# A hybrid decoder step: causal convolution in channel-major projection tiles, and gates and memory queries inside the last tiles

## The chip, the cores and the metric

One core of a Trainium2 chip runs the whole kernel. The time is that of one execution on the device, in microseconds (us). TensorE (PE) multiplies, VectorE (DVE), ScalarE (ACT) and GpSimd (POOL) work on elements, SyncE (SP) only issues transfers; ScalarE and GpSimd issue transfers too. The engines run side by side, each strictly in its own order, and wait for one another by semaphores.

## The reference

One layer of a decoder step, for a prompt of 512 rows and for 32 sample rows (8 sequences of 4 tokens). Cut to what matters here:

```
z = rms_norm(x) @ w_in              # 2048 columns in; split into the groups below
# (A) mLSTM, 4 heads of 256: q and k go through a short convolution over time
m_qk, m_v, m_o, m_gate, m_if = ...  # 2048, 1024, 1024, 1024 and 8 columns
y[t, c] = b[c] + sum_j w[j, c] * m_qk[t - 3 + j, c]     # 4 taps, per channel
qk = silu(y);  p_conv = last 3 rows of m_qk             # an output
ig = m_if[:, :4] + b_if;  lf = log_sigmoid(m_if[:, 4:] + b_if)
# per head: weights of every pair of rows from the running sum of lf and its running
# maximum with ig; num = (q k^T * weights) v + carried state; normalised, * sigmoid(m_o)
# (B) sparse attention, 4 heads of 128, with an index that selects keys per query
# (C) attention into 256 memory tokens, 4 heads of 128: queries c_q, gate c_gate
mix = concat(m_out * silu(m_gate), a_out * silu(a_gate), c_out * silu(c_gate))
out = x + rms_norm(mix @ w_out)
```

The sample rows go through the same with cached keys, memory keys and values (8 sequences of 256 tokens) and carried states.

## The kernel before

**Tiles.** `tensor_tile` makes 512 columns of `z` at a time: two tiles of the memory's keys and values, then the columns behind the mLSTM group (first group), then the 10 tiles of `w_in`'s first 5120 columns (second group, N_B0 to N_Y0: q and k of the convolution in tiles 1 to 4, v 5 and 6, o 7 and 8, gate 9 and 10), and at the end the output projection. A tile has 8 chunks of 256 input rows. For each chunk ScalarE casts the weights to a high part (`w_hi`, L385) when the chunk two before is used, GpSimd makes the low part (`w_lo`, L389), and TensorE adds three products for each k and block of 128 rows (L431 to L433; two for the sample rows, L426 and L427): the rows of x stand, the weights move, so a block is row-major. ScalarE scales the finished blocks by the row's norm and stores them to `z_prompt` and `z_sample` in memory.

**Hosted work.** While TensorE runs the second group it also does the sparse attention. `tensor_prompt` (the prompt's index, selection and attention) and `tensor_gather` (the sample rows; L991 is the row sum) are generators: `tensor_tile` takes a step of `steps[0]` in the middle and at the end of a chunk, and one of `steps[1]` at its end, ahead of that of `steps[0]`. `scalar_tile` does the same once a chunk, behind its cast, one piece behind TensorE. VectorE runs 80 iterations, one for each chunk: a step of the prompt, one of the rows, one of the prompt. The prompt's steps end early in the tenth tile.

**Behind the tiles** comes, in this order: attention into memory for the samples (`*_mem_s`: the queries from `z_sample`, the sum of their two parts at L1348, a cleared `q_spread`, then per sequence key transposes L1397 and logits L1409, softmax, values L1424). `beside_memory` sets the four parts of `*_mlstm_gates` between its steps (i and f transposed, ScalarE's Exp and Ln at L1581 and L1583, VectorE's sums and running maxima L1610 to L1625, and the turn of the convolution's weights). Their constants are loaded by `sync_mlstm_consts`. Next is the convolution of head 0, then what the samples need (`*_mlstm_s_prep`, loads from L1921), then the four heads. In the loop of head h stand also the state pairs of the samples (`side`; in heads 1 to 3) and the four units of the convolution of head h + 1:

```
side(0)
if h + 1 < H:
    tensor_conv_turn(pe, h + 1, i)      # 4 transposes of 128x128 into CONV (L1655)
side(1)
```

A unit is 128 channels by 512 rows. `vector_conv` takes the four taps from PSUM (L1667, L1669), `scalar_conv` the Silu (L1681), each with a table load ahead of it, because the head's other functions stand in another table. `sync_mlstm_head` loads five blocks of 512 KB for each head: q, k, o, gate, v.

Memory key and value pages (512 KB) are loaded by GpSimd (`gpsimd_mem_in`) into three buffers, from the end of the tenth tile on.

## Time and profile before

| what | value |
|---|---|
| median of 3 runs | 1882.44 us (1881.62 to 1884.41) |
| the profiled execution's own time | 1877.01 us |
| its span (first to last instruction) | 1875.3 us |
| mean granted clock of TensorE | 0.937 of full speed |
| TensorE busy | 1679.8 us, 90% |
| VectorE, ScalarE, GpSimd busy | 814.8, 569.1, 673.4 us |

All times of rows are in us from the span's start. The second group runs from about 624 to 1256.4, memory attention to 1325.5, head 0's convolution and the samples' start to 1350.8, the heads from there to 1595, the output projection from 1647.5 to 1845. A row of the timeline has the start, the duration, engine, line and operation, output and inputs, and in brackets how long the engine was idle before and what released it. "x16" counts instructions.

### The profile page before, as it was taken

To read this page: it belongs to the slowest core of one execution; us is meant where nothing else is said; L and a number is where in the kernel's file an instruction comes from. 1 tells how busy PE (TensorE), PEld (TensorE's weight loads), DVE (VectorE), ACT (ScalarE), POOL (GpSimd) and SP (SyncE) were. 2 spreads that over 40 slices of the span, in tenths; PEclk is the share of its full clock that TensorE was granted. 3 is DMA by queue.
4 is the path that set the end of the run, shared out by engine and by line. 5 is a ranking of instruction groups with operands and counts; after the bars stand their busy time and mean duration, and the time that the engine had idled before them with its cause. 6 is when DMAs were issued, how large, how long until landed. Compare 5 with 4: busy or idle time off the path is not lost.

```text
span 1875.3 us, 20980 instructions
## 1 busy us (share of the span) xinstructions
PE 1679.8 (90%) x7801; PEld 1272.0 (68%) x7801; DVE 814.8 (43%) x1319; ACT 569.1 (30%) x876; POOL 673.4 (36%) x448
## 2 busy tenths in 40 slices
PE   6899999999999499998899999987658789799995
PEld 5677775677897376776688778865334455477774
DVE  6400010599929856755632161112465454501113
ACT  5522233222221233233222422224244443312221
POOL 3655531333333166766444444421110111033331
PEclk9999999999999699999999999998667788789997
DMA  6544431233344267766455544437404323542222
GB/s 214 160 134 130 142 101 56 71 105 108 92 120 144 77 196 231 221 197 211 122 154 165 149 134 117 147 125 230 93 29 152 107 68 107 192 160 85 83 78 106
DMA packets 139674, 249.01 MB, mean 133 GB/s; under 512 B 26504, under 2 KB 63308, under 8 KB 136296
## 3 DMA queue, kind: packets, MB, share of 16 engines
q10 hardware_dynamic: 66928, 122.86, 21.0%
q1 hardware_dynamic: 55920, 72.76, 12.2%
q0 software_dynamic: 16736, 52.18, 9.6%
q8 instruction: 58, 0.95, 0.2%
q14 instruction: 32, 0.26, 0.0%
HBM read 204.11 MB, written 43.66 MB: 132 GB/s over the span
## 4 chain that ended last, share of the span: by engine, by line
PE 73%; DVE 13%; DMA 5%; ACT 4%; issue 2%; POOL 1%; ACTq 1%; SPq 0%; DVEq 0%; POOLq 0%
PE acc L431 16%; PE acc L433 16%; PE acc L432 16%; PE acc L426 4%; PE acc L427 4%; PE ps_c L991 3%; PE acc L1722 2%; DVE arena L1669 1%; PE ps_c L2116 1%; PE acc L2111 1%; DMA arena<-z_prompt 1%; PE ps_a L1155 1%; POOL w_lo L389 1%; ACT z_tile L471 1%; PE ps_a L1224 1%
## 5 line engine op out<-in xcount | busy, mean ns | idle before, releaser
L389 POOL TENSOR_TENSOR w_lo<-w_raw,w_hi 128x1024 fp32r<-128x1024 f32 (+1 forms) x200 | 466.7, 2334 | 814.8 <-ACT w_hi L385 814.5
L431 PE MATMUL acc<-w_hi,x_hi 128*128 128x512 f32 (+1 forms) x1472 | 580.4, 394 | 8.8 <-DVE keep L925 5.3
L433 PE MATMUL acc<-w_hi,x_lo 128*128 128x512 f32 (+1 forms) x1472 | 565.9, 384 | 0.0
L432 PE MATMUL acc<-w_lo,x_hi 128*128 128x512 f32 (+1 forms) x1472 | 565.3, 384 | 0.0
L385 ACT CAST w_hi<-w_raw 128x1024 fp32r<-128x1024 f32 (+1 forms) x200 | 204.2, 1021 | 758.3 <-PE acc L427 716.6
L431 PEld LDWEIGHTS acc<-w_hi,x_hi 128*128 128x128 f32 x1472 | 278.8, 189 | 93.9 <-issue 28.0
L433 PEld LDWEIGHTS acc<-w_hi,x_lo 128*128 128x128 f32 x1472 | 278.1, 189 | 55.8
L432 PEld LDWEIGHTS acc<-w_lo,x_hi 128*128 128x128 f32 x1472 | 278.8, 189 | 51.4 <-issue 0.7
L426 PE MATMUL acc<-w_hi,x_hi 128*64 128x512 f32 (+1 forms) x368 | 141.4, 385 | 0.0
L427 PE MATMUL acc<-w_lo,x_hi 128*64 128x512 f32 (+1 forms) x368 | 140.9, 384 | 0.0
L2231 DVE TENSOR_TENSOR arena<-arena (+1 forms) x16 | 14.0, 887 | 176.8 <-ACT arena L464 176.8
L471 ACT ACTIVATE z_tile<-acc,small 128x512 f32<-128x512 f32 (+3 forms) x95 | 63.6, 669 | 48.3 <-PE acc L433 32.1
L881 POOL DMA_INDIRECT arena<-in_cache_attn_k,keep x64 | 67.4, 1054 | 19.5 <-issue 19.5
L795 DVE MAX8 keep<-arena 32x8 f32<-32x2052 f32 x32 | 73.2, 2286 | 1.1
L796 DVE FIND_INDEX8 arena<-keep,arena 32x8 uint32<-32x2052 f32 x32 | 72.9, 2277 | 0.0
L797 DVE MATCH_REPLACE8 arena<-keep,arena 32x2052 f32<-32x2052 f32 x32 | 72.6, 2268 | 0.0
L427 PEld LDWEIGHTS acc<-w_lo,x_hi 128*64 128x64 f32 x368 | 49.5, 134 | 31.5 <-issue 0.2
L657 DVE TENSOR_TENSOR arena<-arena 32x1104 f32<-32x1104 f32 x1 | 1.3, 1297 | 158.3 <-DMA arena<-z_sample 158.3
L881 POOL DMA_INDIRECT arena<-in_cache_attn_v,keep x64 | 62.2, 972 | 14.5 <-issue 11.6
L426 PEld LDWEIGHTS acc<-w_hi,x_hi 128*64 128x64 f32 x368 | 49.5, 135 | 23.6 <-issue 0.2
L991 PEld LDWEIGHTS ps_c<-arena 128*128 128x128 f32 x512 | 62.1, 192 | 4.4
L991 PE MATMUL ps_c<-arena 128*128 128x1 f32 x512 | 58.9, 245 | 0.0
(439 smaller groups left out, 1903.0 us busy)
## 6 DMA issues: line engine op xcount, KB each, us to landing
w_raw<-in_w_in ACTq DMA_DIRECT2D x136, 512.0 KB, 3.7
z_prompt<-z_tile ACTq DMA_DIRECT2D x68, 256.0 KB, 2.5
w_raw<-in_w_out ACTq DMA_DIRECT2D x32, 512.0 KB, 3.6
arena<-z_prompt SPq DMA_DIRECT2D x4, 2088.0 KB, 10.2
w_raw<-in_w_mem_kv ACTq DMA_DIRECT2D x16, 512.0 KB, 4.1
arena<-q_sample POOLq DMA_DIRECT2D x32, 256.0 KB, 4.0
arena<-z_prompt SPq DMA_DIRECT2D x10, 512.0 KB, 7.3
between<-z_prompt SPq DMA_DIRECT2D x10, 512.0 KB, 10.1
```

What stands on the lines that cost most here:

```text
L385: nc.scalar.copy(w_hi[:, c % 2, :, 0:w], w_raw[:, c % RAWS, :, 0:w]).then_inc(chunk_hi, 1)
L389: nc.gpsimd.tensor_tensor(out=w_lo[:, c % 2, :, 0:w], in0=w_raw[:, c % RAWS, :, 0:w], in1=w_hi[:, c % 2, :, 0:w].bitcast(F32), op=ALU.subt ...
L426: nc.tensor.matmul(acc[m][0:2 * R, 0:w], xs, wh, start=first, stop=False)
L427: last = nc.tensor.matmul(acc[m][0:2 * R, 0:w], xs, wl, start=False, stop=end)
L431: nc.tensor.matmul(acc[m][:, 0:w], xh, wh, start=first, stop=False)
L432: nc.tensor.matmul(acc[m][:, 0:w], xh, wl, start=False, stop=False)
L433: last = nc.tensor.matmul(acc[m][:, 0:w], xl, wh, start=False, stop=end)
L471: nc.scalar.activation(z_tile[0:rows, m, 0:w], acc[m][0:rows, 0:w], ACT.Copy, scale=rstd(NU_MEM + m, rows)).then_inc(acc_read, 1)
L795: dlink(nc.vector.max(top8, score))
L796: dlink(nc.vector.max_index(sel_idx[:, 8 * i:8 * i + 8], top8, score))
L881: pool.indirect_dma_start(out=got_v[s][:, c, :], out_offset=None, in_=v_rows if values else k_rows, in_offset=bass.IndirectOffsetOnAxis(ap ...
L991: last = nc.tensor.matmul(ps_c[:, PC_O + h * R + r:PC_O + h * R + r + 1], got_v[s][:, c, h * AD:(h + 1) * AD], probs_t[:, c, h, r:r + 1], ...
```

## The change

It computes the four q and k tiles as fifth to eighth of the second group, and channel-major: the weights stand, x moves, and a block is 128 channels by 512 rows. ScalarE copies such a block and doesn't store it. In the first four iterations of the next tile VectorE scales it by the row norms (broadcast over the partitions by `tensor_late_consts` once, after the third tile of the first group), keeps the last three columns for `p_conv` and applies the taps in place (`vector_conv`). ScalarE takes the four Silu of a tile and stores them to `qk_p` at the seventh chunk (`late`). The heads load q and k from there, and have no convolution any more.

The gates and the sum, transposes and spreading of the memory queries go into the tenth tile: TensorE's first gate part after the second chunk, the queries' transposes after the fourth, the last gate part after the seventh; ScalarE's four parts at its chunks 3, 5, 6 and 8. Their loads are issued by SP as soon as the prompt's attention is stored. VectorE runs the gates, then the queries, then the end of the gathered rows. The first two pages of memory keys go to the buffer of the prompt's memory keys and values, and are issued once GpSimd is done with the casts. The loads of head 0's v, o and gate wait until the memory keys are used, since `q_spread` now lies there. `p_conv` is stored from SBUF in six transfers of single elements.

```diff
+    NCT = 2 * MW // TN
+    B_ORDER = (4, 5, 6, 7, 0, 1, 2, 3, 8, 9)
+    CT0 = B_ORDER.index(0)
...
+        qk_p = scratch("qk_prompt", [2 * MW, S])
...
-                return w_in_v, TN * (n - N_B0)
+                return w_in_v, TN * B_ORDER[n - N_B0]
...
+                            if kind == "t":
+                                xh, xl = hi_t[:, k, 0:S], lo_t[:, k, :]
+                                wh, wl = (v[:, c % 2, i, m * P:(m + 1) * P] for v in (w_hi, w_lo))
+                                nc.tensor.matmul(acc[m][:, :], wh, xh, start=first, stop=False)
+                                nc.tensor.matmul(acc[m][:, :], wl, xh, start=False, stop=False)
+                                last = nc.tensor.matmul(acc[m][:, :], wh, xl, start=False, stop=end)
+                                continue
...
+                if kind == "t" and m < MT:
+                    nc.scalar.copy(z_tile[:, m, :], acc[m][:, :]).then_inc(acc_read, 1)
+                    continue
...
+                if c == CH - 2 and late is not None:
+                    late()
...
+            for dst, src in ((conv_nat[0:CK, :], I["conv_w"][0]), (conv_nat[CK:CK + 1, :], I["conv_b"][0:1, :])):
+                sp.dma_start(dst, src).then_inc(tables_in, 16)
...
+        def tensor_late_consts(pe):
+            pe.wait_ge(*at("rstd_spread"))
+            pe.wait_ge(tables_in, 16 * N_TABLES)
+            for m in range(MT):
+                nc.tensor.matmul(ps_c[:, m * P:(m + 1) * P], conv_a[:, m * P:(m + 1) * P], ident[:, :], start=True, stop=True)
+            for k in range(KT):
+                last = nc.tensor.transpose(ps_b[:, k * (CK + 1):(k + 1) * (CK + 1)], conv_nat[:, k * P:(k + 1) * P],
+                                           ident[0:CK + 1, 0:CK + 1])
+            last.then_inc(reached("late_turned"), 1)
+
+        def vector_late_consts(dve):
+            dve.wait_ge(rstd_ready, 2)
+            for m in range(MT):
+                last = nc.vector.tensor_copy(conv_a[:, m * P:(m + 1) * P], rstd(NU_MEM + m, P).broadcast_to([P, P]))
+            last.then_inc(reached("rstd_spread"), 1)
+            dve.wait_ge(*at("late_turned"))
+            nc.vector.tensor_copy(rstd_bc, ps_c[:, :])
+            nc.vector.tensor_copy(conv_c, ps_b[:, 0:KT * (CK + 1)].rearrange("p (k j) -> p k j", j=CK + 1)
+                                  ).then_inc(reached("late_copied"), 1)
+            dve.wait_ge(*at("late_copied"))
...
+        def vector_conv(dve, i, m):
+
+            k = 4 * i + m
+            dve.wait_ge(acc_read, acc_base(N_B0 + CT0 + i) + m + 1)
+            dlink(nc.vector.tensor_tensor(out=conv_a, in0=z_tile[:, m, :], in1=rstd_bc, op=ALU.mult))
+            nc.vector.tensor_copy(last_rows(k // 8)[:, k % 8, :], conv_a[:, S - CK + 1:S])
+            out = z_tile[:, m, :]
+            dlink(nc.vector.tensor_scalar(out, conv_a, conv_c[:, k, CK - 1:CK], None, ALU.mult))
+            for j in range(1, CK):
+                ins = nc.vector.scalar_tensor_tensor(out=out[:, j:S], in0=conv_a[:, 0:S - j],
+                                                     scalar=conv_c[:, k, CK - 1 - j:CK - j], in1=out[:, j:S],
+                                                     op0=ALU.mult, op1=ALU.add)
+                if j < CK - 1:
+                    dlink(ins)
+            ins.then_inc(cv_tapped, 1)
+            dve.wait_ge(cv_tapped, k + 1)
+
+        def scalar_conv(act, i):
+
+            for m in range(MT):
+                k = 4 * i + m
+                act.wait_ge(cv_tapped, k + 1)
+                nc.scalar.activation(z_tile[:, m, :], z_tile[:, m, :], ACT.Silu, bias=conv_c[:, k, CK:CK + 1]).then_inc(cv_silu, 1)
+            for m in range(MT):
+                k = 4 * i + m
+                act.wait_ge(cv_silu, k + 1)
+                act.dma_start(qk_p[k * P:(k + 1) * P, :], z_tile[:, m, :]).then_inc(z_stored[m], 16)
 
...
+        cq_in = place(X_OFF, [2, AW], R)
+        cq_low = place(10 * (S + R) + 13324, [2, AW], R)
+        q_spread = place(10 * (S + R), [H * NB * (P + NQ)])
+        k_mem = [mem_kv[:, :, 0:AW], mem_kv[:, :, AW:2 * AW], part(xh_free, 4224, [NMEM // P, AW])]
...
 
         def gpsimd_mem_in(pool):
-            pool.wait_ge(chunk_used, CH * N_Y0)
-            pool.dma_start(cq_in, z_s[0:R, C_CQ:C_CQ + 2 * AW].rearrange("r (a c) -> r a c", a=2)).then_inc(cq_loaded, 16)
-            pool.dma_start(cq_low, z_s[R:2 * R, C_CQ:C_CQ + 2 * AW].rearrange("r (a c) -> r a c", a=2)).then_inc(cq_loaded, 16)
+            pool.wait_ge(o_stored, 16 * 2 * MT)
+            pool.wait_ge(mem_out, 16 * 2 * NMEM // P)
             for i in range(2 * NB):
                 b = i % NB
+                if i == 2:
+                    pool.wait_ge(chunk_used, CH * N_Y0)
...
             dve.wait_ge(cq_loaded, 32)
-            for m in range(MT + 1):
-                dve.wait_ge(z_stored[m], 16 * (N_Y0 - N_A0))
             nc.vector.tensor_tensor(out=cq_in, in0=cq_in, in1=cq_low, op=ALU.add).then_inc(reached("cq_ready"), 1)
-            nc.vector.memset(q_spread, 0.0)
-            for t in range(2):
-                dlink(nc.vector.memset(p_spread[t], 0.0))
+            dlink(nc.vector.memset(q_spread, 0.0))
             dve.wait_ge(*at("cq_ready"))
             for h in range(H):
                 last = nc.vector.tensor_copy(gate_c[h * R:(h + 1) * R, :], cq_in[:, 1, h * AD:(h + 1) * AD])
@@ -1357,6 +1430,10 @@
             nc.vector.tensor_copy(q_spread.rearrange("p (i x) -> p i x", x=P + NQ)[:, :, 0:NQ],
...
+            for m in range(MT + 1):
+                dve.wait_ge(z_stored[m], 16 * (N_Y0 - N_A0))
+            for t in range(2):
+                dlink(nc.vector.memset(p_spread[t], 0.0))
...
         def tensor_mem_s(pe):
             pe.wait_ge(*at("cq_ready"))
+            pe.wait_ge(g_copied, 5)
             for h in range(H):
                 last = nc.tensor.transpose(ps_a[:, h * R:(h + 1) * R], cq_in[:, 0, h * AD:(h + 1) * AD], ident[0:R, 0:R])
...
+            pe.wait_ge(*at("g_cols"))
...
+                if b == 0:
+                    pe.wait_ge(*at("mixed_s"))
...
-            act.wait_ge(*at("gate_c_in"))
-            nc.scalar.activation(gate_c, gate_c, ACT.Silu).then_inc(reached("gate_c_ready"), 1)
-            yield
...
+            act.wait_ge(*at("gate_c_in"))
+            nc.scalar.activation(gate_c, gate_c, ACT.Silu).then_inc(reached("gate_c_ready"), 1)
...
+        head_rows = sb("head_rows", [P, H * P])
+        hr = head_rows[0:H, :]
+        rstd_bc = head_rows[:, :]
+
+        z_h = [place(M0, [2, MT, MD]), part(xl_free, 0, [2, MT, MD])]
...
 
         def sync_mlstm_consts(sp):
-            sp.wait_ge(mix_stored, 16 * H)
             sp.wait_ge(o_stored, 16 * 2 * MT)
             sp.wait_ge(kv_stored, 48 * MT)
-            for i in range(MT + 1):
-                sp.wait_ge(z_stored[i], 16 * (N_Y0 - N_A0))
+            sp.wait_ge(cv_tapped, 4 * NCT)
+            sp.dma_start(cq_in, z_s[0:R, C_CQ:C_CQ + 2 * AW].rearrange("r (a c) -> r a c", a=2)).then_inc(cq_loaded, 16)
+            sp.dma_start(cq_low, z_s[R:2 * R, C_CQ:C_CQ + 2 * AW].rearrange("r (a c) -> r a c", a=2)).then_inc(cq_loaded, 16)
...
                              (batch_of, C["batch_of"]), (causal, C["causal"]),
-                             (hn, I["mlstm_head_norm"][0:1, :].broadcast_to([P, MW])),
-                             (conv_nat[0:CK, :], I["conv_w"][0]), (conv_nat[CK:CK + 1, :], I["conv_b"][0:1, :]),
                              (ifp, z_p[:, C_IF:C_IF + 2 * H].rearrange("(m p) c -> p m c", p=P)),
...
-            sp.dma_start(O["p_conv"].rearrange("l b j c -> (l b j) c"), z_p[S - CK + 1:S, 0:2 * MW]).then_inc(conv_out, 16)
+
+        def sync_conv_state(sp):
+            sp.wait_ge(cv_tapped, 4 * NCT)
+            for half in range(2):
+                for j in range(CK - 1):
+                    sp.dma_start(O["p_conv"][0, 0, j, half * MW:(half + 1) * MW].rearrange("(k p) -> p k", p=P),
+                                 last_rows(half)[:, :, j], allow_slow_non_contiguous=True).then_inc(conv_out, 16)
...
         def sync_mlstm_head(sp, h):
             if h == 0:
-                sp.wait_ge(chunk_used, CH * N_Y0)
+                sp.wait_ge(*at("mixed_s"))
+                for i in range(MT + 1):
+                    sp.wait_ge(z_stored[i], 16 * (N_Y0 - N_A0))
             if h >= 2:
                 sp.wait_ge(c_done, 2 * (h - 1))
                 sp.wait_ge(h_out, h - 1)
-            for i, c in enumerate((C_QK, C_QK + MW, C_O, C_G, C_V)):
+            for i in range(2):
+                src = qk_p[i * MW + h * MD:i * MW + (h + 1) * MD, :].rearrange("(d p) t -> p d t", p=P)
+                sp.dma_start(qk_t[h % 2][:, i, :, :], src).then_inc(zh_in[h % 2], 16)
+            if h == 0:
+                sp.wait_ge(cl_used, NB)
+                sp.dma_start(hn, I["mlstm_head_norm"][0:1, :].broadcast_to([P, MW])).then_inc(hn_in, 16)
+            for i, c in enumerate((C_V, C_O, C_G)):
                 src = z_p[:, c + h * MD:c + (h + 1) * MD].rearrange("(m p) c -> p m c", p=P)
-                dst = va[h % 2][:, :, 0:MD] if i == 4 else z_h[h % 2][:, i, :, :]
+                dst = va[h % 2][:, :, 0:MD] if i == 0 else z_h[h % 2][:, i - 1, :, :]
                 sp.dma_start(dst, src).then_inc(zh_in[h % 2], 16)
 
...
-        GATES = acc[0:3]
+        GATES = (ps_a, ps_b, ps_a)
...
+            pe.wait_ge(g_copied, 1)
...
-            pe.wait_ge(g_copied, 5)
-            for k in range(KT):
-                last = nc.tensor.transpose(GATES[0][:, k * (CK + 1):(k + 1) * (CK + 1)], conv_nat[:, k * P:(k + 1) * P],
-                                           ident[0:CK + 1, 0:CK + 1])
-            last.then_inc(reached("conv_w_t"), 1)
-            yield
...
-            pe.wait_ge(conv_silu, 4 * (h + 1))
+            pe.wait_ge(zh_in[h % 2], zh_count(h))
...
-                if h + 1 < H:
-                    tensor_conv_turn(pe, h + 1, i)
...
-                if h + 1 < H:
-                    vector_conv(dve, h + 1, i)
...
-                if h + 1 < H:
-                    scalar_conv(act, h + 1, i)
...
+        def tile_kind(n):
+            return "t" if B_ORDER[n - N_B0] < NCT else "b"
...
+        GATE_GAPS = (4, 3, 3)
+
+        def spaced(pieces, gaps):
+
+            next(pieces)
+            for g in gaps:
+                yield from hosted_pause(g)
+                next(pieces)
+            yield from pieces
...
                 sync_prompt_out(sp, m)
+            sync_mlstm_consts(sp)
+            sync_conv_state(sp)
             sp.wait_ge(*at("mixed_s"))
             store_mix_s(sp, o_s, MW)
-            sync_mlstm_consts(sp)
...
-            steps = (chain(hosted_pause(1), scalar_prompt(act)), chain(hosted_pause(1), scalar_gather(act)))
+            steps = (chain(hosted_pause(1), scalar_prompt(act), hosted_pause(2), spaced(scalar_mlstm_gates(act), GATE_GAPS)),
+                     chain(hosted_pause(1), scalar_gather(act)))
             for n in range(N_B0, N_Y0):
-                scalar_tile(act, n, "b", steps)
+                i = n - N_B0
+                scalar_tile(act, n, tile_kind(n), steps,
+                            late=(lambda i=i: scalar_conv(act, i - CT0 - 1)) if CT0 < i <= CT0 + NCT else None)
             run(steps[0])
             run(steps[1])
-            beside_memory(scalar_mem_s(act), scalar_mlstm_gates(act), (4, 6, 8, 9))
-            for u in range(4):
-                scalar_conv(act, 0, u)
+            run(scalar_mem_s(act))
...
-            for _ in range(CH * NBT):
+            for i in range(CH * NBT):
                 next(prompt, None)
                 next(rows, None)
                 next(prompt, None)
+                t = i // CH - CT0 - 1
+                if 0 <= t < NCT and i % CH < MT:
+                    vector_conv(dve, t, i % CH)
             run(prompt)
             run(rows)
-            vector_gather_out(dve)
+            vector_mlstm_gates(dve)
             mem_s = vector_mem_s(dve)
             next(mem_s)
-            vector_mlstm_gates(dve)
+            vector_gather_out(dve)
             run(mem_s)
-            for u in range(4):
-                vector_conv(dve, 0, u)
             prep, pairs = vector_mlstm_s_prep(dve), vector_mlstm_s(dve)
             next(prep)
             for h in range(H):
...
+            tensor_late_consts(pe)
...
-            steps = (tensor_prompt(pe), chain(tensor_rows(pe), tensor_gather(pe)))
+            mem_s = tensor_mem_s(pe)
+            gates = tensor_mlstm_gates(pe)
+
+            def gates_and_queries():
+                next(gates)
+                yield from hosted_pause(GATE_GAPS[0])
+                next(mem_s)
+                yield from hosted_pause(sum(GATE_GAPS[1:]))
+                yield from gates
+            steps = (chain(tensor_prompt(pe), hosted_pause(2), gates_and_queries()), chain(tensor_rows(pe), tensor_gather(pe)))
             for n in range(N_B0, N_Y0):
-                tensor_tile(pe, n, "b", steps)
+                tensor_tile(pe, n, tile_kind(n), steps)
             run(steps[0])
             run(steps[1])
             tensor_gather_out(pe)
-            beside_memory(tensor_mem_s(pe), tensor_mlstm_gates(pe), (4, 6, 9))
-            for u in range(4):
-                tensor_conv_turn(pe, 0, u)
+            run(mem_s)
```

## Rows read from the trace of the kernel before

**Rows 1.** The page, part 4: the chain, shares by engine

```profile
PE 73%; DVE 13%; DMA 5%; ACT 4%; issue 2%; POOL 1%; ACTq 1%; SPq 0%; DVEq 0%; POOLq 0%
```

**Rows 2.** Stretches behind the tiles: busy time of each engine, clock, transfers

```profile
core 0: us, PE busy (x) PEld busy (x) DVE busy (x) ACT busy (x) POOL busy (x), PEclk, DMA share, GB/s
1256.40:1269.80 13.40, 0.87 (x6) 0.50 (x5) 9.88 (x15) 2.27 (x3) 3.29 (x5) 0.70 0.55 185
1269.80:1305.00 35.20, 29.82 (x173) 24.71 (x173) 8.81 (x22) 19.30 (x41) 5.69 (x8) 0.87 0.85 285
...
1325.50:1350.80 25.30, 11.35 (x26) 5.25 (x26) 17.56 (x21) 5.85 (x9) 0.00 (x0) 0.53 0.44 64
1350.80:1391.10 40.30, 18.37 (x111) 14.29 (x112) 24.47 (x53) 18.20 (x21) 3.57 (x9) 0.58 0.17 52
1406.40:1461.00 54.60, 40.49 (x147) 22.10 (x147) 32.43 (x65) 23.42 (x39) 0.00 (x0) 0.80 0.45 140
1476.30:1529.60 53.30, 40.01 (x143) 21.36 (x143) 31.21 (x61) 23.26 (x39) 0.00 (x0) 0.79 0.45 143
1544.70:1580.30 35.60, 30.55 (x127) 15.90 (x127) 19.82 (x45) 13.65 (x29) 0.00 (x0) 0.94 0.46 140
```

**Rows 3.** Groups by line and shape on VectorE, 1325 to 1600

```profile
L1667 DVE TENSOR_SCALAR arena<-acc,keep_m 128x512 f32<-128x512 f32 x16 | 12.0, 750 | 33.8 <-PE acc L1655 33.7
L1669 DVE SCALAR_TENSOR_TENSOR arena<-acc,keep_m,arena 128x511 f32<-128x511 f32 x16 | 12.0, 750 | 0.6
```

**Rows 4.** Timeline of the gate chain and of the sum of the queries

```profile
1291.30 0.66 ACT L1581 ACTIVATE arena<-arena 4x544 f32<-4x544 f32 x1
1291.97 1.28 ACT L1583 ACT_TABLE_LOAD   x1
...
1293.96 0.71 DVE L1610 SCALAR_TENSOR_TENSOR arena<-arena 4x544 f32<-4x544 f32 x1 [9.10 <-ACT arena L1583]
...
1299.91 0.15 DVE L1625 TENSOR_TENSOR keep_m<-keep_m,arena 4x8 f32<-4x8 f32 x1
...
1260.53 1.21 DVE L1348 TENSOR_TENSOR between<-between 32x1024 f32<-32x1024 f32 x1 [1.62 <-DMA z_sample<-z_tile]
```

**Rows 5.** The sample's loads: issue, time to landing, VectorE's wait

```profile
1328.44 0.33 SPq L1921 DMA_DIRECT2D between<-z_sample  x1
...
between<-z_sample SPq DMA_DIRECT2D x1, 640.0 KB, 9.7
...
1347.94 2.81 DVE L1967 TENSOR_TENSOR between<-between,z_tile 32x2560 f32<-32x2560 f32 x1 [3.69 <-DMA z_tile<-z_sample]
```

**Rows 6.** Timeline of the tenth tile: row sum, ScalarE's next cast

```profile
1227.23 1.84 PE L991 MATMUL ps_c<-arena 128*128 128x1 f32 x16
...
1227.84 1.04 ACT L385 CAST w_hi<-w_raw 128x1024 fp32r<-128x1024 f32 x1 [7.14 <-PE acc L427]
```

**Rows 7.** Waits in the ten tiles: total, times, longest

```profile
DVE keep_p L1275 <- PE ps_c L1232: 66.9, 23, 4.3
...
DVE arena L1288 <- PE ps_a L1224: 43.8, 4, 25.5
```

**Rows 8.** TensorE behind a stall, and the granted clock there

```profile
922.96 0.80 PE L431 MATMUL acc<-w_hi,x_hi 128*128 128x512 f32 x1 [5.25 <-DVE keep L925]
...
924.00:926.00 2.00, 2.00 (x6) 1.61 (x5) 1.86 (x7) 0.00 (x0) 0.27 (x1) 0.50 0.69 199
926.00:928.00 2.00, 2.00 (x7) 1.57 (x7) 1.90 (x5) 0.00 (x0) 0.00 (x0) 0.68 0.08 33
```

**Rows 9.** Waits in head 1

```profile
PE acc L1655 <- DMA arena<-z_prompt: 3.7, 1, 3.7
```

**Rows 10.** Timeline of L1186 with and without a GpSimd cast

```profile
726.99 0.48 DVE L1186 SCALAR_TENSOR_TENSOR arena<-arena,keep_p 128x256 f32<-128x256 f32 x1
...
730.47 2.96 DVE L1186 SCALAR_TENSOR_TENSOR arena<-arena,keep_p 128x256 f32<-128x256 f32 x2 [0.48 <-ACT arena L1168]
...
730.24 2.39 POOL L389 TENSOR_TENSOR w_lo<-w_raw,w_hi 128x1024 fp32r<-128x1024 f32 x1 [2.32 <-ACT w_hi L385]
```

More of the change, by code:

```diff
@@ L58, in hybrid_decoder_step @@
     NBT = C_IF // TN
+    NCT = 2 * MW // TN
+    B_ORDER = (4, 5, 6, 7, 0, 1, 2, 3, 8, 9)
+    CT0 = B_ORDER.index(0)
+    assert len(B_ORDER) == NBT and B_ORDER[CT0:CT0 + NCT] == tuple(range(NCT))
     N_Y0 = N_B0 + NBT
@@ L566, in hybrid_decoder_step @@
         gate_s = keep[:, 912:1040]
+        CK = 4
+        conv_nat = place(X_OFF, [2 * MW], CK + 1)
+        conv_a = place(X_OFF + 3112, [S])
+        conv_c = conv_cols[:, :].rearrange("p (k j) -> p k j", j=CK + 1)
+        last_rows = lambda half: small[:, 32 * half:32 * half + 24].rearrange("p (k j) -> p k j", j=CK - 1)
         POOL_PAGES = 2 * CH * IXT
@@ L1315, in part @@
                                                   **dict(zip(names, shape)))
-        cq_in, cq_low = (part(between, X_HI_N + X_LO_N + i * W_N + W_N // 2, [2, AW])[0:R] for i in range(2))
-        q_spread = part(xh_free, 0, [H * NB * (P + NQ)])
-        k_mem = [part(xh_free, 4224, [NMEM // P, AW]), part(xh_free, 5248, [NMEM // P, AW]),
-                 w_raw[:, RAWS - 1, :, :]]
+        cq_in = place(X_OFF, [2, AW], R)
+        cq_low = place(10 * (S + R) + 13324, [2, AW], R)
+        q_spread = place(10 * (S + R), [H * NB * (P + NQ)])
+        k_mem = [mem_kv[:, :, 0:AW], mem_kv[:, :, AW:2 * AW], part(xh_free, 4224, [NMEM // P, AW])]
         KS = len(k_mem)
@@ L1324, in hybrid_decoder_step @@
         o_c = part(xh_free, 8320 + 2 * NMEM, [AD])
-        gate_c = part(xh_free, 8320 + 2 * NMEM + AD, [AD])
+        gate_c = place(10 * (S + R) + H * NB * (P + NQ), [AD])
         p_spread = [part(zt_free, i * 1056, [NB * (P + NQ)]) for i in range(2)]
@@ L1462, in hybrid_decoder_step @@
         c_e = keep_m[:, 40:60].rearrange("p (m h) -> p m h", h=H)
[L1463 to L1475 removed]
+        mx_T = keep_m[0:H, 60:70]
+        bias_g = keep_m[0:H, 70:72]
+        m0_s = keep_m[0:H, 72:80]
+        a_T = keep_m[0:H, 80:88]
+        bn_o = keep_m[:, 88:96]
+        st_m = keep_m[:, 96:104]
+        aT8 = keep_m[0:NB, 104:108]
+        w_b = keep_m[0:R, 108:140].rearrange("p (h b) -> p h b", h=H)
+        batch_of = keep_m[0:R, 140:148]
+        head_rows = sb("head_rows", [P, H * P])
+        hr = head_rows[0:H, :]
+        rstd_bc = head_rows[:, :]
+        z_h = [place(M0, [2, MT, MD]), part(xl_free, 0, [2, MT, MD])]
         va = [place(M0 + 5120, [MT, MD + 2]), part(xl_free, 4096, [MT, MD + 2])]
         qk_t = [place(M0 + 7180, [2, 2, S]), part(xl_free, 5128, [2, 2, S])]
[L1478 removed]
         k_n = place(M0 + 9228, [MT, MD])
@@ L1488, in hybrid_decoder_step @@
         n_o = place(M0 + 14860, [MD], 1)
-        causal = place(M0 + 15116, [P])
+        causal = place(M0 + 6152, [P])
         assert M0 + 15244 <= AR_N
-        conv_nat = place(M0 + 10252, [2 * MW], CK + 1)
         ifp = place(M0 + 12300, [MT, 2 * H])
@@ L1494, in hybrid_decoder_step @@
         m0_nat = place(M0 + 12396, [H], NB)
-        (mc_in, xc_turned, xc_done, kn_turned, kn_done) = (
-            sem(n) for n in ("mc_in", "xc_turned", "xc_done", "kn_turned", "kn_done"))
+        (mc_in, kn_turned, kn_done) = (
+            sem(n) for n in ("mc_in", "kn_turned", "kn_done"))
         (g_turned, g_copied, mb_done, w_arg, w_exp, s_done, w_done, h_done, gates_mixed, h_sqrt,
@@ L1576, in scalar_mlstm_gates @@
             yield
-            act.wait_ge(*at("conv_w_t"))
-            nc.scalar.copy(conv_c, GATES[0][:, 0:KT * (CK + 1)].rearrange("p (k j) -> p k j", j=CK + 1)).then_inc(reached("conv_w_c"), 1)
             act.wait_ge(*at("g_abs"))
@@ L1804, in vector_mlstm_head @@
             dve.wait_ge(gates_mixed, 2 * (h + 1))
-            nc.vector.tensor_tensor(out=h_o, in0=h_o, in1=z_h[h % 2][:, 2, :, :], op=ALU.mult).then_inc(h_out, 1)
-        conv_silu = sem("conv_silu")
+            nc.vector.tensor_tensor(out=h_o, in0=h_o, in1=z_h[h % 2][:, 0, :, :], op=ALU.mult).then_inc(h_out, 1)
         var_m = sem("var_m")
@@ L2264, in run @@
                 pass
-        def beside_memory(mem_s, gates, places):
-            for i, _ in enumerate(mem_s):
-                if i in places:
-                    next(gates)
-            run(gates)
+        GATE_GAPS = (4, 3, 3)
[5 more added lines that the diff above has]
+            yield from pieces
         def beside_head(h, prep, pairs):
@@ L2453, in _ @@
             vector_rstd(dve, NU_MEM, NU_NORM)
+            vector_late_consts(dve)
             vector_index_prep(dve)
```

98 lines of the change are left out of this document (25 added, 73 removed).

## The prediction

> **What bounds the kernel now.** I read the views in this order: the chain that ended last, the stretches behind the tiles, the operations in them, then waits and single operations.
>
> The chain is TensorE's for 73% of the span and VectorE's for 13% [rows 1]. In the input-projection tiles TensorE is never idle for long, so anything added there on TensorE, or waited for there, is paid in full. From the end of the tenth tile (1256.4 us) to 1580 it is different [rows 2]. In the first 13.4 us TensorE works 0.87 us: it waits for the store of the sample rows, the queries' load and a clearing. In the 25.3 us from 1325.5 it works 11.4, VectorE 17.6. Heads 1 and 2 (each cut from its first product, L1691, to its L1722, the products with v) take 54.6 and 53.3 us; head 3, which has no next head to convolve, takes 35.6, with as many bytes per us and the same two state pairs beside it. The difference is the convolution: each unit has one L1667 and three L1669 on VectorE, 0.75 us each [rows 3], 3.0 us, between transposes and a Silu with a table load. The granted clock is .53 and .58 in the two stretches up to 1391 and .94 in head 3.
>
> **What the change takes out behind the tiles.**
>
> *Memory attention.* The first key transposes can start at the tile's end, since queries and two pages are there: 13.4 us earlier. In the keys and the softmax (35.2 us to 1305) stands the gate chain, now in the last tile. I take 8 us for it and for the two pages already in: the operations of [rows 4] from Exp to L1625 run in this stretch. Against this, value pages will meet the loads of the heads, which are now held until the keys are done. Least: the 13.4 alone. Most: 13.4 + 15.6, the 35.2 cut to the 19.3 that ScalarE is busy in it. I take -21.5 (-13 to -29).
>
> *Head 0's convolution and the sample's start.* The convolution from 1325.5 (25.3 less the 9.3 below: 16 us) goes, but not its time. The loads of the sample's rows are issued at 1328.4, 2.9 us behind the end of memory attention, and take 9.7 us [rows 5]; today they land under the convolution. Then come two VectorE products of 2.8 with a load between them (3.7 waited): 9.3. So 2.9 + 9.7 + about 1.6 for what is issued behind (a load one us later) + 9.3 = 23.5, against 25.3: -1.8 (0 to -9, if the loads land in the 3.7).
>
> *Head 0.* Its stretch from 1350.8 to L1722, 40.3 us, hosts four units of head 1. Each puts 3.0 us on VectorE and one ScalarE table load of 1.28 [rows 4] on the exchange: 4 x 4.3 = -17.3 (-12 by VectorE alone, -25 if transposes, Silu and load back count too).
>
> *Heads 1 and 2* become head 3: 54.6 - 35.6 = -19.0 and 53.3 - 35.6 = -17.7 (-12 each, by VectorE alone). Head 3, the last pairs and the output tiles stay.
>
> Sum: -77.3.
>
> **What it puts into the tiles.**
>
> *The products themselves.* A channel-major tile has the same three products per k and block, at the same width: 0. The order of tiles alone: 0.
>
> *Constants after the third tile.* 20 small products. Sixteen one-column products of L991 take 1.84 us [rows 6]; 20 at that price are +2.3.
>
> *Convolution, 16 units.* Per unit a product, a first tap and three more taps, each 512 wide (0.75 at that width, [rows 3]), and a copy of three columns: about 3.8 us of VectorE, four in each of four tiles, behind the second prompt step of an iteration. Tiles six and eight have the idle time after top-k: VectorE waits there 43.8 us in four waits [rows 7], against 8 x 3.8 = 30. In the other two tiles VectorE waits for TensorE once in each attention step, 66.9 us in 23 waits, 2.9 each [rows 7], and the unit mostly fits. ScalarE's four Silu and stores come at the seventh chunk, some 7 us with two loads, and ScalarE stands idle 7.14 ahead of a cast [rows 6]. Only in the last such tile do they fall amid an attention step: +2.5 for all of it (0 to 20).
>
> *Gates, first part* (end of the second chunk of the last tile): eleven transposes at 0.115 and a turn to ScalarE and back (0.66): +2.5 (1 to 4).
>
> *Memory queries* (end of the fourth chunk). TensorE must wait for the queries' sum, which stands on VectorE behind all of the gate chain, and that behind Ln on ScalarE, which is issued behind the cast that waits for this very chunk. In times of before: the cast ends at 1228.9 [rows 6], Exp 0.66, load 1.28, Ln 0.66 [rows 4], to 1231.5; VectorE's L1610 to L1625 from 1293.96 to 1300.06, 6.1; the sum 1.21: 1238.8. TensorE has the row sum until 1228.9 as cover. So it stands +10 us (0 if the order came out otherwise, 13 with an Exp load). Behind it wait the next chunk and, through it, ScalarE's casts and GpSimd's; nothing in that chain is needed by the wait, so there is no deadlock. Four transposes: +0.6. Gates' last part: ten, +1.1.
>
> *Clock.* After a stall of 5.25 us in an earlier tile TensorE was back at 922.96, with a granted clock of .50, the 1.2 GHz level, until 926 and of .68 in the two us to 928, so 1.00 from about 927.3 [rows 8]: 4.3 us at half, 2.2 lost. After the 10 us above: +2.5 (2 to 5).
>
> Sum: +21.5. GpSimd's page issues and SP's constants, queries and six stores of the convolution's state are moved into the tenth tile, where both queues stand idle; the price of SP's stores of single elements isn't in the trace, but the heads' loads behind them wait for the tile's end anyway: 0.
>
> **Sum.** 1877.0 - 77.3 + 21.5 = 1821.2 for an execution like the profiled one. The median of the runs shown is 5.4 above that: 1827.
>
> **The rivals.** Main case as above, 1827.
>
> *A: the stall is hidden* (VectorE and ScalarE come out ahead of TensorE at the fourth chunk). 12.5 less: 1814. Against it: the cast waits for that chunk by its order.
>
> *B: heads don't become head 3.* Another exchange (state pairs, ScalarE's table loads, or the next head's loads, for which head 1 waits 3.7 us even now [rows 9]) fills what the convolution leaves. Half of the heads' 54.0 us is lost: 1854. For it: head 3 loads nothing for a next head, so its length leaves that out.
>
> *C: VectorE is slowed by GpSimd in the tiles.* Two L1186 that began just behind a GpSimd cast took 2.96 us; one without it took 0.48 [rows 10]. The last three taps and the scaling read two operands from SBUF as L1186 does, where the old taps read PSUM. If each unit in the two tiles of attention takes one such block (2.96 - 2 x 0.48 = 2.0), it is 5.8 us long, against an idle time of 2.9: 8 x 2.9 = 23 us come to TensorE, so 1850. The Trainium skill, "SBUF — State Buffer", section "Who interferes with whom", says that a VectorE instruction with two SBUF inputs contends with a GpSimd instruction that reads SBUF, and it would speak against the new place of the taps; the two L1186 agree.
>
> *D, the other side: the units stand on TensorE's path.* An iteration's next prompt step waits behind the unit on VectorE, and TensorE waits for it in every hosted piece. Then 16 x 3.8 = 61 us come into the tiles, with the block of C 16 x 5.8 = 93: 1888 to 1920, and the change is slower. It decides from 55.8/16 = 3.5 us of each unit on. For it: VectorE runs in order. Against it: the 43.8 us of idle time cover half of the units.
>
> That the change doesn't do what it says would mean that the heads keep their length altogether (B in full, 54 us lost: 1881, no change).
>
> **How the numbers follow.** Main .46, A .14, B .18 and in full .03, C .11, D .08. A measurement of this kernel tells 0.2% (3.8 us) from no change. Faster: main, A, B, C: .89; same .03; slower .08. The range runs from 1804 (A with the larger gain in memory attention) to 1862 (beyond B and C), and leaves out D, B in full and the corners.
>
> **What the profile after would show.** No transposes and taps in the heads; L1691 to L1722 near 36 us in heads 1 and 2, and a higher clock there. First key transposes at the tile's end, memory attention done some 48 us behind it. In the tenth tile one TensorE wait of about 10 us for the queries' sum, at half clock behind it. Taps of 0.7 in tiles six to nine, some of them 2 us and more beside a cast. The prediction is wrong if tiles six to nine grow by more than 10 us together, if the heads stay above 45, or if the fourth chunk shows no wait.

## The result, and the profile after

The changed kernel takes 1836.45 us (four runs, 1833.49 to 1841.48) against 1883.43 (1881.62 to 1886.33): a ratio of 0.9752, 95% interval 0.9723 to 0.9781. The prediction was 1827, with 1804 to 1862, so it is inside the range and 9 us above the likeliest value. The profiled execution took 1841.48 us, its span 1839.8. Line numbers after the change are higher: L390 is ScalarE's cast (L385 before), L1463 transposes the queries, L1423 is their sum, L1732 a head's first product (L1691 before), L1761 the products with v (L1722), L1604 the stores of the convolution's state.

The stretches that answer to [rows 2], cut at the same events: end of the tenth tile, first value product, end of memory attention, first product of the samples, head 0's L1761, then heads 1, 2 and 3 from L1732 to L1761.

```profile
core 0: us, PE busy (x) PEld busy (x) DVE busy (x) ACT busy (x) POOL busy (x), PEclk, DMA share, GB/s
1288.00:1313.90 25.90, 22.02 (x132) 18.76 (x130) 5.56 (x14) 10.93 (x20) 6.51 (x9) 1.00 0.80 262
1313.90:1338.20 24.30, 19.04 (x38) 7.41 (x38) 1.51 (x6) 0.54 (x2) 3.61 (x5) 0.86 0.83 284
1338.20:1361.90 23.70, 4.70 (x9) 1.68 (x8) 5.59 (x3) 2.96 (x5) 0.00 (x0) 0.53 0.47 68
1361.90:1387.70 25.80, 15.91 (x94) 12.59 (x94) 13.45 (x37) 12.77 (x16) 3.57 (x9) 0.58 0.27 81
1401.30:1438.60 37.30, 32.28 (x130) 16.83 (x130) 21.11 (x50) 13.67 (x29) 0.00 (x0) 0.91 0.64 204
1452.70:1494.40 41.70, 36.62 (x127) 18.45 (x127) 19.86 (x45) 13.73 (x29) 0.00 (x0) 0.78 0.59 183
1509.60:1545.20 35.60, 30.57 (x126) 15.85 (x126) 19.83 (x45) 13.59 (x29) 0.00 (x0) 0.94 0.45 140
```

Against before: memory attention takes 50.2 us from the tile's end (69.1 before: 13.4, 35.2, and 20.5 for the values to 1325.5), the samples' start 23.7 (25.3), head 0 25.8 (40.3), head 1 37.3 (54.6), head 2 41.7 (53.3), head 3 the same. With the stretches between heads (1.7 and 1.2 shorter) the tail wins 66.8 us. The tenth tile ends at 1288.0 in place of 1256.4, so the tiles and what is ahead of them give back 31.6. The rest, 35.2, is nearly all of the 35.5 us between the spans of the two profiled executions. The medians are 47 apart: this execution is 5 above its median, that of before 6 below.

Where they give it back is in TensorE's waits; a wait has its sum, count and longest:

```profile
PE ps_a L1463 <- DVE arena L1423: 15.0, 1, 15.0
...
PE acc L439 <- DVE keep L1001: 10.7, 1, 10.7
...
PE ps_a L1636 <- DVE arena L1687: 2.4, 1, 2.4
```

The first is the predicted wait for the queries' sum, 15.0 us in place of 10. The second stood at 5.25 before [rows 8]. The timelines of ScalarE, SP and TensorE around the first:

```profile
1246.66 1.04 ACT L390 CAST w_hi<-w_raw 128x1024 fp32r<-128x1024 f32 x1 [12.50 <-DMA w_raw<-in_w_in]
1247.61 0.65 ACT L1663 ACTIVATE arena<-arena 4x544 f32<-4x544 f32 x1
...
1216.43 29.84 SPq L1604 DMA_DIRECT2D out_p_conv<-small  x6
...
1257.56 0.64 PE L1463 MATMUL ps_a<-ident,arena 32*128 32x32 f32 x4 [15.03 <-DVE arena L1423]
```

The cast ahead of Exp waits for its weights, where that of [rows 6] waited for TensorE, while SP is 29.84 us at six stores of 4 KB each. In these us (the transfers' view of 1216 to 1248: packets, MB, share of 16 engines; then KB and us to landing) weights land 18.6 us after they were asked for; 3.7 is the median of the whole profile:

```profile
q1 hardware_dynamic: 5020, 0.13, 28.1%
...
w_raw<-in_w_in ACTq DMA_DIRECT2D x3, 512.0 KB, 18.6
```

### The profile page after: what moved, and what is told of

Same layout as the page of the kernel before. It is cut to its first block, busy times and chain, and to the rows that moved or that the text cites. A ratio compares the mean times of both kernels' runs of the same rounds, so it can differ in the third digit from the quotient of the medians.

```text
span 1839.8 us, 20894 instructions
## 1 busy us (share of the span) xinstructions
PE 1654.7 (90%) x7745; PEld 1255.5 (68%) x7745; DVE 833.1 (45%) x1357; ACT 546.4 (30%) x860; POOL 677.4 (37%) x446
## 3 DMA queue, kind: packets, MB, share of 16 engines
q0 software_dynamic: 16640, 51.92, 10.1%
## 4 chain that ended last, share of the span: by engine, by line
PE 75%; DVE 13%; DMA 5%; ACT 3%; issue 2%; ACTq 1%; POOL 1%; SPq 0%; DVEq 0%; POOLq 0%
PE acc L443 14%; PE acc L445 13%; PE acc L444 13%; PE acc L431 4%; PE acc L432 4%; PE ps_c L1067 3%; PE acc L439 2%; PE acc L441 2%; PE acc L440 2%; PE acc L2146 2%; PE ps_c L2151 2%; DMA w_raw<-in_w_in 1%; PE acc L1761 1%; DMA arena<-z_prompt 1%; PE ps_a L1750 1%
## 5 line engine op out<-in xcount | busy, mean ns | idle before, releaser
L443 PE MATMUL acc<-w_hi,x_hi 128*128 128x512 f32 (+1 forms) x1216 | 475.3, 391 | 2.8 <-POOL w_lo L394 1.9
L445 PE MATMUL acc<-w_hi,x_lo 128*128 128x512 f32 (+1 forms) x1216 | 465.4, 383 | 0.0
L444 PE MATMUL acc<-w_lo,x_hi 128*128 128x512 f32 (+1 forms) x1216 | 464.9, 382 | 0.0
L390 ACT CAST w_hi<-w_raw 128x1024 fp32r<-128x1024 f32 (+1 forms) x200 | 204.2, 1021 | 768.7 <-PE acc L432 714.6
L443 PEld LDWEIGHTS acc<-w_hi,x_hi 128*128 128x128 f32 x1216 | 230.6, 190 | 67.4 <-issue 17.6
L445 PEld LDWEIGHTS acc<-w_hi,x_lo 128*128 128x128 f32 x1216 | 229.8, 189 | 45.1
L444 PEld LDWEIGHTS acc<-w_lo,x_hi 128*128 128x128 f32 x1216 | 230.2, 189 | 42.3 <-issue 0.7
L439 PE MATMUL acc<-x_hi,w_hi 128*128 128x512 f32 x256 | 105.7, 413 | 11.8 <-DVE keep L1001 10.7
L441 PE MATMUL acc<-x_lo,w_hi 128*128 128x512 f32 x256 | 100.8, 394 | 0.0
L440 PE MATMUL acc<-x_hi,w_lo 128*128 128x512 f32 x256 | 100.8, 394 | 0.0
L957 POOL DMA_INDIRECT arena<-in_cache_attn_v,keep x64 | 65.8, 1028 | 14.5 <-issue 10.8
L439 PEld LDWEIGHTS acc<-x_hi,w_hi 128*128 128x128 f32 x256 | 48.9, 191 | 32.1 <-DVE keep L1001 11.0
```

The costliest lines, as they stand in the source:

```text
L390: nc.scalar.copy(w_hi[:, c % 2, :, 0:w], w_raw[:, c % RAWS, :, 0:w]).then_inc(chunk_hi, 1)
L439: nc.tensor.matmul(acc[m][:, :], wh, xh, start=first, stop=False)
L440: nc.tensor.matmul(acc[m][:, :], wl, xh, start=False, stop=False)
L441: last = nc.tensor.matmul(acc[m][:, :], wh, xl, start=False, stop=end)
L443: nc.tensor.matmul(acc[m][:, 0:w], xh, wh, start=first, stop=False)
L444: nc.tensor.matmul(acc[m][:, 0:w], xh, wl, start=False, stop=False)
```

## The experiments

Each time is a median of five runs (four for the stores in tile nine), beside the kernel before on the same chip. The changed kernel was run again as a measure: ratio 0.9769 (0.9751 to 0.9787).

**The changed kernel again.**

> The changed kernel as it is, as the measure for the other three of this call. Its four times so far were 1833.5, 1833.7, 1839.2 and 1841.5 us; in the execution shown head 2 had a granted clock of .78 over 41.7 us, against .94 over 35.6 in head 3, with the same waits. Theory: the upper times are those with such a long stretch at half clock, about 6 us. Then executions fall near 1834 or near 1840, and one near 1834 shows head 2 at some 36 us. Rival: head 2 is always 41.7 long, and the spread comes from elsewhere.

1838.51 us (1836.77 to 1842.44). Its profile shows the wait for the queries' sum at 11.6 us, where the first profile of the same kernel has 15.0; the cast ahead of it waits 9.1 us for its weights (12.5), and SP is 26.8 us at the six stores (29.84):

```profile
PE ps_a L1463 <- DVE arena L1423: 11.6, 1, 11.6
```

Head 2 is at 41.7 us once more. In four later profiles heads 1 and 2, from one L1732 to the next, took: 51.3 and 50.9 (stores behind the state loads), 57.6 and 51.1 (queries later), 51.4 and 56.8 (both), 52.7 and 51.3 (head 1's loads later). So a head is 5 to 6 us longer in some, now the one and now the other. In the changed kernel's head 2 (windows):

```profile
1455.00:1463.00 8.00, 6.70 (x12) 2.85 (x13) 3.00 (x5) 3.64 (x7) 0.00 (x0) 0.53 0.74 237
1463.00:1471.00 8.00, 8.00 (x20) 3.45 (x19) 2.33 (x5) 1.20 (x3) 0.00 (x0) 0.50 0.79 266
```

From 1457.4 on TensorE is busy all the time and waits for nothing, but stays at the 1.2 GHz level (0.50), as a head's start leaves it, until some 1472. That is some 17 us of half clock, where head 3 has 3.4, and it accounts for the 6 us. The upper times aren't explained by it: this kernel's five runs don't fall into two groups.

**The stores elsewhere.** Behind the sample's state loads:

```diff
-            sync_mlstm_consts(sp)
-            sync_conv_state(sp)
+            sync_mlstm_consts(sp)
...
             sync_mlstm_s(sp)
+            sync_conv_state(sp)
```

> The six stores of the convolution's state (6144 elements of 4 bytes) go behind the sample's state loads, out of the tenth tile. Theory 1: these stores hold up the weights' and constants' transfers; the cast in the fifth chunk's turn no longer waits for its weights, the wait for the queries' sum falls from 15.0 to about 9.6 us and the 2.4 us wait for the gates' constants goes: 5 to 8 us less, unless the stores then hold up head 1 or its state pairs. Rival: the wait of 15.0 is that of the gate chain alone and stays: no change.

1831.36 us, 7.2 less (0.9733). The cast doesn't wait for weights, the 2.4 us for the gates' constants are gone, and the wait is what the prediction's sum had:

```profile
PE ps_a L1463 <- DVE arena L1423: 9.7, 1, 9.7
```

From the fourth chunk's cast to that of the next tile's first, the last tile took 39.1 us before, 61.3 in the changed kernel (58.9 in its second profile) and 52.4 here: 13.3 for gates and queries, where the prediction had 15.6, and 8.9 (6.5) for the stores. Ahead of the prompt's last outputs instead (`if m == MT - 1: sync_conv_state(sp)` before `sync_prompt_out(sp, m)`):

> The six stores go ahead of the last outputs of the prompt's attention, so into the eighth or ninth tile, where no wait hangs on a transfer. Theory 1: 5 to 8 us less, as in the run beside it, if weights that are asked for two chunks ahead outlast the jam of some 30 us; if not, the casts there wait for their weights by some 5 us and nothing is gained. Rival (the wait is the gate chain's alone): no change.

1859.88 us, 21.4 more: theory 1 and the rival both miss. Weights hold a cast only 4.5 us, and the wait for the queries' sum is 9.7 here too. But SP stands at the stores, the prompt's outputs queue behind them, VectorE waits for these, and TensorE for VectorE. SP's timeline, then the waits:

```profile
1165.01 30.40 SPq L1604 DMA_DIRECT2D out_p_conv<-small  x6
1195.45 38.25 SPq L1377 DMA_DIRECT2D mix_prompt<-arena  x2
```

```profile
DVE keep_p L1351 <- DMA mix_prompt<-arena: 23.0, 1, 23.0
...
PE ps_c L1308 <- DVE arena L1353: 16.4, 1, 16.4
```

So the stores cost by what they hold up, transfers and SP's queue, and the place decides.

**The queries two chunks later** (the fourth pause longer by 4 pieces, the next shorter by 4):

```diff
-                yield from hosted_pause(GATE_GAPS[0])
+                yield from hosted_pause(GATE_GAPS[0] + 4)
                 next(mem_s)
-                yield from hosted_pause(sum(GATE_GAPS[1:]))
+                yield from hosted_pause(sum(GATE_GAPS[1:]) - 4)
```

> TensorE takes the queries' transposes at the end of the sixth chunk of the last tile instead of the fourth. Theory: the wait is only one of order, the gate chain runs under the two chunks, and the 15.0 us go, with some 2.5 us of half clock behind them: 15 to 18 us less. Rival: the chain's own cast or the weights behind the stores hold TensorE in the fifth or sixth chunk instead, and half or less is gained (0 to 8 us).

1829.73 us, 8.8 less (0.9714). The wait for the sum is gone, as it was one of order; but now the casts wait for weights behind the stores, and only half of what the theory forecast is gained. The rival had this mechanism, with 0 to 8 us:

```profile
ACT w_hi L390 <- DMA w_raw<-in_w_in: 18.0, 2, 14.5
```

**Both.**

> The stores behind the state loads and the queries two chunks later. With the stores alone the wait for the queries' sum was 9.7 us, as in the prediction's sum; with the queries later alone it was gone, but casts waited 18.0 us for weights. Theory: the two add up; no wait above 3 us in the last tile, 9.7 and some 2.5 us of half clock less than with the stores alone: 1819 (1816 to 1822). Rival: something else in the last tile (the gates' parts, ScalarE's order) holds TensorE now: 1826 to 1831.

1821.55 us, 0.9684 (0.9663 to 0.9705): 17 less than the changed kernel, and no wait above 2 us in the last tile, which takes 41.3 us by the measure above (39.1 before the change). The two add up.

**The units in the tiles.** First their place: two units at the end of the third and of the fourth iteration, `if 0 <= t < NCT and i % CH in (2, 3)`.

> Two convolution units each in the third and fourth iteration of a tile, instead of one in each of the first four. In the sixth tile TensorE waits 10.7 us for the sample rows' maximum (5.3 before the change), with two units ahead of it on VectorE. Theory: these two are the cause; the wait falls to 5 to 6 us, and the tiles are 5 us shorter, unless two units in a row hold another step: then it comes back as a wait there. Rival: the units delay VectorE wherever they stand, no change.

1848.87 us, 10.4 more (0.9836). TensorE's waits in the sixth tile, and a new one in the seventh:

```profile
PE acc L439 <- DVE arena L1007: 8.9, 1, 8.9
PE acc L439 <- DVE keep L1001: 5.3, 1, 5.3
PE ps_c L1067 <- DVE arena L1353: 2.5, 1, 2.5
```

The wait for the maximum (L1001) is back at 5.3, so the two units ahead of it were its cause. But four units now stand ahead of the step behind it (L1007), which waits 8.9 where the changed kernel waits 1.1. So the theory's exception came true, and the rival's "no change" misses by 10 us: the place of the units matters, and those iterations of the sixth tile have no slack for them. Then their taps left out:

```diff
-            dlink(nc.vector.tensor_scalar(out, conv_a, conv_c[:, k, CK - 1:CK], None, ALU.mult))
-            for j in range(1, CK):
...
-            ins.then_inc(cv_tapped, 1)
+            nc.vector.tensor_copy(out[:, 0:8], conv_a[:, 0:8]).then_inc(cv_tapped, 1)
```

> The units keep their order and their waits, but scale and copy only 8 columns and apply no taps: q and k stay unconvolved and the kept last columns are others. It tells what VectorE's work in the tiles costs. Theory: the 5.4 us of the longer wait in the sixth tile go, and nothing else; 4 to 7 us less than the changed kernel. Rival (the units stand on TensorE's path): 3.5 us and more for each, 40 us and more less.

1831.68 us, 6.8 less by medians, 4.5 by the ratios (0.9745), whose intervals meet. The wait in the sixth tile is 6.2. Units on TensorE's path throughout would have given 40 and more.

**The kernel before without the convolution** (heads load blocks of the same size in place of the convolved q and k, all calls of the three functions removed):

```diff
-                if h + 1 < H:
-                    vector_conv(dve, h + 1, i)
...
-            for u in range(4):
-                vector_conv(dve, 0, u)
```

> The kernel before, with the convolution of q and k left out everywhere: the heads load blocks of the same size where the convolved q and k stood. It is the tail's part of the change without what was put into the tiles. The prediction's terms: the convolution of head 0 gives only 1.8 us (the sample's loads take its place), heads 0 to 2 give 17.3, 19.0 and 17.7, 55.8 in all: about 1827. By the measured rows of the changed kernel (1.6, 14.5 + 1.7, 17.3 + 1.2, 11.6 or 17.7): 48 to 54. Rival: the 16 us of head 0's convolution count in full: 70.

1829.75 us, 51.6 less (0.9739), inside the 48 to 54. The windows of the samples' start (from the end of memory attention, here 1327.3) and of heads 0, 1 and 2:

```profile
1327.30:1350.10 22.80, 3.70 (x8) 1.25 (x9) 5.65 (x4) 1.68 (x4) 0.00 (x0) 0.57 0.47 71
1350.10:1376.10 26.00, 17.14 (x94) 13.37 (x94) 13.67 (x37) 13.06 (x16) 3.57 (x9) 0.50 0.26 80
1391.40:1427.00 35.60, 31.13 (x130) 16.47 (x130) 18.55 (x46) 12.98 (x29) 0.00 (x0) 0.94 0.67 214
1442.80:1478.00 35.20, 30.52 (x126) 15.88 (x126) 19.51 (x45) 13.19 (x30) 0.00 (x0) 0.94 0.70 217
```

Without its 16 us of convolution the samples' start is 22.8 us long, only 2.5 less, and memory attention ahead of it ends 1.8 later than before. So the rival of 70 falls. Head 0 is 14.3 shorter, and heads 1 and 2 are head 3.

**The loads around memory attention**, on the kernel with both. Head 1's loads behind the state loads (`sync_mlstm_head(sp, 1)` after `sync_mlstm_s(sp)`):

> On the kernel with both (stores behind the state loads, queries two chunks later; 1821.6 us): the loads of head 1 go behind the sample's state loads, out of the memory values. In the changed kernel the values took 24.3 us, 20.5 before, with the heads' loads beside them at up to 388 GB/s. Theory: the collision is the missing part of the memory term; values back to 20 to 21, 3 to 4 us less, 1818, and head 1 not held up. Rival: head 0's own loads are enough of a collision, or head 1 waits for its loads: no change.

1819.3 us (0.9685), near the 1818 of the theory. The sample's large load, mask and small stores ahead of head 1's loads, the third page buffer in `w_raw[:, RAWS - 1, :, :]`:

> On the kernel with both: the third page buffer of the memory keys goes to a free weight buffer, so that the sample's large load (640 KB), the small mask and the two small stores of the maxima can be issued ahead of head 1's loads, under memory attention; the second part (320 KB) stays behind it. Theory: the stretch from the end of memory attention to the sample's first product (24.6 us) is set by these loads, not by the convolution that stood there; now 2.4 + some 7 + 9.3 = 18.7, 6 us less: 1816. Rival: the second part takes as long by itself, or the loads only add to the collision in the values: within 2 us of 1821.6.

1819.14 us (0.9678), where the theory had 1816. The two together:

> The two edits of this call together, on the kernel with both: sample's loads under memory attention, head 1's loads behind the state loads. Theory: 3 to 4 and 6 add up, 1812. Rival: the sample's load takes the place of head 1's in the collision, and the values stay long: 1816.

1818.66 us (0.9666): the two don't add up to the 1812 of the theory, and the values take 24.0 us, as the rival had it. And the sample's load held back by `sp.wait_ge(cv_done, NB - 3)`:

> The kernel with both loads moved, and the sample's large load waits until the last memory value page has been asked for (five sequences' values used). With that load ahead of head 1's the values took 30.3 us, with head 1's loads later 18.9, with both 24.0; the stretch behind them 17.6 in place of 24.6. Theory: the sample's load collides with the value pages; held back, the values go to 19 to 20 us and the stretch behind them grows by some 3: 2 to 4 us less, 1815. Rival: what the values win the stretch behind loses: 1818 to 1819.

1817.38 us (0.9656, 0.9633 to 0.9679). No one of the four is clear of the kernel with both by its interval, but the stages show what moved. The windows of the values, with head 1's loads later and with the sample's load early:

```profile
1293.90:1312.80 18.90, 17.00 (x33) 6.24 (x33) 0.00 (x0) 0.51 (x2) 3.61 (x5) 0.91 0.72 227
```

```profile
1291.00:1321.30 30.30, 18.28 (x33) 7.32 (x34) 0.00 (x1) 0.46 (x2) 3.61 (x5) 0.77 0.83 250
```

With both the values took 23.3: 4.4 less with head 1's loads gone, as expected, 7.0 more with the sample's load beside them. The stretch behind, from the last value product to the sample's first, went from 24.5 (1317.0 to 1341.6) to 17.6 (1321.2 to 1338.8), as the theory had. What the one wins the other loses. In the last kernel the values took 25.6 and the stretch 17.7: the rival's side, with a theory of 19 to 20 missed. Its median is the lowest of all, 63 us under the kernel before and 21 under the changed one; that it is 4.2 under the kernel with both, the intervals don't settle.

## Why the prediction was right, and what its terms missed

- *Heads* (54.0 forecast). In the profiled execution 14.5, 17.3 and 11.6, 43.4 in all; with the convolution simply left out 14.3, 19.0 and 18.1, 51.4. Heads 1 and 2 do become head 3: 35.6 and 35.2 there. Head 2's shortfall in the changed kernel is a stretch at half clock. Rival B falls. Head 0's term was 2.8 too large; the bound below it, 12 by VectorE alone, held.
- *Samples' start* (1.8): 1.6, and 2.5 without the convolution. The step was right: these loads take the convolution's place, and moved ahead they give 7 us there.
- *Memory attention* (21.5): 18.9. The loads of the heads beside the values, named as the reason for the middle value, cost 3.8 us there (24.3 against 20.5).
- *Constants*: 2.3 forecast. Casts in the first group come 1.6 to 1.9 us later than before ahead of them (by 1.6 already at 134.7, far ahead of the constants) and 4.0 behind: 2.1.
- *Units* (2.5): from 4.0 late at the second group's start to 8.3 at its ninth tile's end, 4.3; within one chunk of the sixth tile the casts go from 0.9 to 6.2 late, and without taps 4.5 to 6.8 are won. The step that failed is "Tiles six and eight have the idle time after top-k". The sample rows' maximum stands behind two units of tile six, on the same engine, and the idle time comes only behind all four: at that tile's end, where it is as long as before. The longest wait of the 43.8 us stands in tile nine, not eight; there it is 11.3 us shorter, the length of three units. VectorE's timeline before, then after:

```profile
964.37 0.56 DVE L1288 SCALAR_TENSOR_TENSOR arena<-ps_a,arena 128x384 f32<-128x384 f32 x1 [14.71 <-PE ps_a L1224]
1147.21 0.69 DVE L1288 SCALAR_TENSOR_TENSOR arena<-ps_a,arena 128x512 f32<-128x512 f32 x1 [25.50 <-PE ps_a L1224]
```

```profile
971.10 0.56 DVE L1364 SCALAR_TENSOR_TENSOR arena<-ps_a,arena 128x384 f32<-128x384 f32 x1 [14.69 <-PE ps_a L1300]
1153.94 0.69 DVE L1364 SCALAR_TENSOR_TENSOR arena<-ps_a,arena 128x512 f32<-128x512 f32 x1 [14.18 <-PE ps_a L1300]
```

  Rival D falls, though VectorE's order is what it was about. Rival C is small over the tiles: a later tap takes 0.75 us from SBUF too (the first one 0.48), and the blocked ones show in the means of the groups by shape (15 of the 16 units):

```profile
L709 DVE SCALAR_TENSOR_TENSOR z_tile<-arena,conv_cols,z_tile 128x510 f32<-128x510 f32 x15 | 13.3, 884 | 0.5
L704 DVE TENSOR_TENSOR arena<-z_tile,head_rows 128x512 f32<-128x512 f32 x15 | 11.5, 766 | 0.3
```

  Over 0.75 and 0.69 unblocked that is 0.13 x 15 + 0.08 x 15 = 3 us of VectorE, and one copy of the last three columns, 0.17 us in the other units, is 2 us longer beside a GpSimd cast. A block in every unit of two tiles was 8 x 2.0 = 16. But this copy is in the second unit ahead of the sixth tile's maximum, and VectorE is not idle from there on, so by the timeline some 2 of that wait's extra 5.4 us are rival C's (no run tests it by itself):

```profile
920.01 2.66 POOL L394 TENSOR_TENSOR w_lo<-w_raw,w_hi 128x1024 fp32r<-128x1024 f32 x1 [2.91 <-ACT w_hi L390]
920.51 2.19 DVE L705 COPY small<-arena 128x3 f32<-128x3 f32 x1
```

- *Gates and queries* (15.6 with the clock, ahead of their last part): 13.3 once the stores are away, with the wait of 9.7 for the 10 forecast. Rival A, that the wait is hidden, falls.
- *The stores: 0 forecast, 6.5 to 9 measured* (7.2 between the medians, 8.9 and 6.5 by the last tile's length in two profiles of the changed kernel). This is the term that the prediction missed. It saw that no instruction of the path waits for these stores and that SP is idle, and costed them at nothing, though it had no row for them; it didn't ask which transfers they stand beside. Weights for the sixth chunk came late, behind them Exp, and with it the wait that was already there. The Trainium skill, "DMA: Bandwidth & Descriptors", section "Issuing engines are not separate DMA queues", says that transfers issued by different engines run on the same 16 DMA engines and interleave; here 18.6 us for weights on ScalarE's queue beside SP's stores agree.

None of the prediction's three signs of being wrong came: tiles six to nine grew by 5.8 us together, no head stayed above 45, and the fourth chunk shows its wait. With the stores at 7 the prediction's sum would have been 1834, and the measured median is 1836.45. That they come so close is in part luck: in the two profiled executions the part behind the tiles won 10.5 us less than forecast (66.8 against 77.3) and the tiles took 10.1 more (31.6 against 21.5), and these 20 us are 9 between the medians only because the two executions lie on opposite sides of theirs. What stays open: why ten of the thirteen profiles with heads free of the convolution have one head with some 13 us more of half clock, and what spreads the executions of one kernel over some 8 us.

## What to carry to other kernels

Moving work under a busy engine pays when what it leaves behind has no second bound: here the heads' exchange was all convolution, but the samples' start had loads of the same length under it. A step set amid a strictly ordered stream must be placed by the order in which its inputs come on every engine, casts included: two chunks later the same transposes were free. And a transfer that nobody waits for still has a price in the transfers beside it and in its queue: look there before writing 0.

## What the runs showed of the hardware that was not expected

Six stores of 1024 elements of 4 bytes, 24 KB in all, took SP 29.8 us to issue beside weight loads (26.8 in a second profile) and 13.6 us behind the state loads, and weights of 512 KB that land in 3.7 us took 18.6 beside them. TensorE stayed at the 1.2 GHz level for some 17 us in one head, busy for nearly all of it, where it was back at 2.4 GHz 4.3 us after the stall of [rows 8]. A VectorE copy of 128x3 elements took 2.19 us beside a GpSimd cast, and 0.17 in the other 15 units.
